# A delta-rule recurrence inside the passes of a two-block kernel: carried by a linear map of each chunk, or by three dependent products

## What is computed

```python
def rwkv7_scan(r, w, k, v, kk, bb, s0, reverse):
    def step(s, inp):
        r_t, w_t, k_t, v_t, kk_t, b_t = inp
        sa = jnp.einsum('bhij,bhj->bhi', s, kk_t)
        s = s * w_t[:, :, None, :] - sa[..., None] * b_t[:, :, None, :] + v_t[..., None] * k_t[:, :, None, :]
        return s, jnp.einsum('bhij,bhj->bhi', s, r_t)
    xs = tuple(jnp.moveaxis(t, 1, 0) for t in (r, w, k, v, kk, bb))
    s, ys = lax.scan(step, s0, xs, reverse=reverse)
    return s, jnp.moveaxis(ys, 0, 1)
```

## Time and profile before

| | us |
|---|---|
| median of three runs (3537.45 to 3548.29) | 3542.62 |
| the profiled execution, its own time | 3542.76 |
| its span | 3541.0 |
| the 12 passes, from the first product of pass 0 to the stage behind them | 660.46 |
| pass 0 | 45.03 |
| an even pass with a recurrence beside it (pass 4) | 55.42 |
| an odd one (pass 5) | 57.42 |
| pass 11 | 48.79 |

### The profile page before, as it was taken

The page is one execution under the profiler, slowest core; times in us unless marked ns, Lnnn a source line. Parts: engine busy times, 40 slices in busy tenths (PEclk is TensorE's granted clock), DMA queues, the critical chain, the costliest instruction groups (busy, mean ns, idle before and its releaser), DMA issues. The chain is left out here.

```text
span 3541.0 us, 67559 instructions
## 1 busy us (share of the span) xinstructions
PE 3073.0 (87%) x28976; PEld 2438.8 (69%) x28976; DVE 1957.7 (55%) x2743; ACT 1120.2 (32%) x1797; POOL 1042.0 (29%) x608
## 2 busy tenths in 40 slices
PE   6898898999699988999939985999999977399886
PEld 3675476887576556787828873888888856289534
DVE  3588757881287874887047703666666541421252
ACT  3223434332323443333241212343333312422222
POOL 0332133554242213454402211443434301032101
PEclk8999999999898999999969997999999988699988
DMA  9332132333232112233313321000000021121102
GB/s 351 97 93 55 32 93 71 96 95 92 61 95 73 53 49 78 84 96 91 96 46 96 109 66 74 17 21 21 3 21 21 8 81 48 39 75 60 42 1 72
DMA packets 345078, 245.48 MB, mean 69 GB/s; under 512 B 9982, under 2 KB 320948, under 8 KB 344008
## 3 DMA queue, kind: packets, MB, share of 16 engines
q1 hardware_dynamic: 340356, 231.44, 21.6%
q10 hardware_dynamic: 4420, 9.66, 0.8%
HBM read 222.27 MB, written 17.23 MB: 68 GB/s over the span
## 5 line engine op out<-in xcount | busy, mean ns | idle before, releaser
L602 POOL TENSOR_TENSOR weights_lo<-weights_raw,weights_hi 128x1024 fp32r<-128x1024 f32 (+1 forms) x234 | 593.3, 2536 | 1114.0 <-ACT weights_hi L571 1114.0
L1200 PE MATMUL psum<-moving_hi,weights_hi 128*128 128x512 f32 x1472 | 601.3, 409 | 73.4 <-DVE weights_lo L602 45.7
L1200 PE MATMUL psum<-moving_lo,weights_hi 128*128 128x512 f32 x1472 | 582.7, 396 | 0.0
L1200 PE MATMUL psum<-moving_hi,weights_lo 128*128 128x512 f32 x1472 | 582.0, 395 | 0.0
L1200 PEld LDWEIGHTS psum<-moving_hi,weights_hi 128*128 128x128 f32 x1472 | 281.6, 191 | 186.7 <-issue 60.8
L571 ACT ACTIVATE weights_hi<-weights_raw 128x1024 fp32r<-128x1024 f32 (+2 forms) x250 | 252.9, 1016 | 245.8 <-PE psum L1200 240.9
L1200 PEld LDWEIGHTS psum<-moving_hi,weights_lo 128*128 128x128 f32 x1472 | 282.0, 192 | 61.3
L1200 PEld LDWEIGHTS psum<-moving_lo,weights_hi 128*128 128x128 f32 x1472 | 282.6, 192 | 57.2 <-issue 3.8
L2632 POOL TENSOR_TENSOR second_off<-second_mats,second_masks 128x256 f32<-128x256 f32 x180 | 141.1, 786 | 183.0 <-PE psum L2077 183.0
L1200 PE MATMUL psum<-hn_hi,even_hi 128*128 128x256 f32 (+1 forms) x480 | 162.4, 338 | 27.2 <-DVE even_lo L602 27.2
L2077 PE MATMUL psum<-second_wb,second_y 64*64 64x64 f32 x2880 | 164.9, 218 | 0.0
(11 more groups left out here) (457 smaller groups left out, 6687.5 us busy)
## 6 DMA issues: line engine op xcount, KB each, us to landing
weights_raw<-in_w_up SPq DMA_DIRECT2D x88, 512.0 KB, 3.9
weights_raw<-in_w_in SPq DMA_DIRECT2D x80, 512.0 KB, 3.8
start_ada<-in_ada_w SPq DMA_DIRECT2D x12, 2048.0 KB, 18.2
odd_raw<-in_od_w_in SPq DMA_DIRECT2D x16, 1024.0 KB, 5.3
even_raw<-in_ev_w_in SPq DMA_DIRECT2D x30, 512.0 KB, 3.9
weights_raw<-in_w_down SPq DMA_DIRECT2D x32, 448.0 KB, 3.9
weights_raw<-in_w_o SPq DMA_DIRECT2D x16, 512.0 KB, 4.3
weights_raw<-in_w_down SPq DMA_DIRECT2D x16, 512.0 KB, 4.2
```

What stands on the lines that cost most here:

```text
L602: ops.tensor_tensor(self.ring.lo[i % n][:, a:b], self.ring.raw[:, t % self.ring.landing, a:b], self.ring.hi[i % n][:, a:b].bitcast(F32), A ...
L1200: return nc.tensor.matmul(to, (hi, lo)[which][:, at:at + P], moving(k)[part], start=start and k == 0 and i == 0, stop=stop and k == n_k - ...
```

## The change

The linear maps go. A new class `Steps` takes the place of `Recurrence` inside the passes. For each chunk k it has four turns, of which three hold work:

- "p": PE makes N v plus (a state) into a 64-column region, ACT first writes the state times the decay into `scaled`, then copies p out (into `wau`, as `p_sb`).
- "u": PE multiplies `wb` with `p_sb`; ACT copies the result (`u_sb`).
- "s": PE makes the new part of the state from v and `u_sb` (two products), and the output `y` (three products, one of them with the old state). DVE makes the next state by one operation with decay and `scaled`; after each fourth chunk it adds `y` into `o`.
- the fourth turn is empty.

The 48 turns are spread over slots: one after each unit, and two for each round, the first between the off-diagonal product and the place of the terms (called A below), the second behind the products of the round before (B). A pass of 15 units has 47 slots, one of 12 units has 44. So one chunk takes four slots, that is four units or two rounds. The unit "a" is made in pass 11 alone, since the `Recurrence` that still runs alone behind the passes needs it; the condition of POOL's wait is put in other words for that. Places of the terms do not move relative to the rounds; among the units they do, as there are fewer.

```diff
--- before.py
+++ after.py
@@ -2227,6 +2227,93 @@
         return range(self.items * place // places, self.items * (place + 1) // places)
 
 
+class Steps:
...
+    def pe(self, pe, what, k):
+        b, nc = self.buf, self.nc
+        n = self.order[k]
+        slot, v, g = slot_of(self.i, n), b.v_tok[:, self.i // 2 % 2, n, :], k // 4
+        state, ar = b.st[:, k % 2, :], b.ar[:, self.i % 3, n, :]
+        if what == "p":
+            if k:
+                pe.wait_ge(self.state_ready, k)
+            last = halves_matmul(nc, self.p, b.ntrk[:, slot, 0:CH], v, start=True, stop=k == 0)
+            if k:
+                last = halves_matmul(nc, self.p, ar[:, 0:CH], state, start=False, stop=True)
+            last.then_inc(self.p_ready, 1)
+        elif what == "u":
+            pe.wait_ge(self.p_taken, k + 1)
+            halves_matmul(nc, self.u, b.wb[:, slot, 0:CH], self.p_sb).then_inc(self.u_ready, 1)
+        else:
+            pe.wait_ge(self.u_taken, k + 1)
+            if k + 1 < NCH:
+                halves_matmul(nc, self.s, b.mats[:, slot, 3 * CH:], v, start=True, stop=False)
+                halves_matmul(nc, self.s, b.mats[:, slot, 2 * CH:3 * CH], self.u_sb, start=False, stop=True).then_inc(self.s_ready, 1)
+            if k % 4 == 0 and g:
+                pe.wait_ge(self.o_added, g)
+            c = n - self.starts[g]
+            y = self.y[:, c * CH:(c + 1) * CH]
+            halves_matmul(nc, y, v, b.ntrk[:, slot, CH:], start=True, stop=False)
+            if k:
+                halves_matmul(nc, y, state, ar[:, CH:], start=False, stop=False)
+            last = halves_matmul(nc, y, self.u_sb, b.mats[:, slot, CH:2 * CH], start=False, stop=True)
+            if k % 4 == 3:
+                last.then_inc(self.out_ready, 1)
+    def act(self, act, what, k):
+        b, S = self.buf, self.nc.scalar
+        if what == "p":
+            if k:
+                n = self.order[k]
+                act.wait_ge(self.state_ready, k)
+                S.activation(self.scaled, b.st[:, k % 2, :], ACT.Identity, scale=b.decay[:, self.i % 3, n:n + 1]).then_inc(self.state_scaled, 1)
+            act.wait_ge(self.p_ready, k + 1)
+            S.activation(self.p_sb, self.p, ACT.Identity).then_inc(self.p_taken, 1)
+        elif what == "u":
+            act.wait_ge(self.u_ready, k + 1)
+            S.activation(self.u_sb, self.u, ACT.Identity).then_inc(self.u_taken, 1)
+    def dve(self, dve, what, k):
+        b, V = self.buf, self.nc.vector
+        if what != "s":
+            return
+        n, g = self.order[k], k // 4
+        decay = b.decay[:, self.i % 3, n:n + 1]
+        if k + 1 < NCH:
+            dve.wait_ge(self.s_ready, k + 1)
+            if k:
+                dve.wait_ge(self.state_scaled, k)
+                V.scalar_tensor_tensor(b.st[:, (k + 1) % 2, :], self.s, decay, self.scaled, ALU.mult, ALU.add).then_inc(self.state_ready, 1)
+            else:
+                V.tensor_scalar(b.st[:, 1, :], self.s, decay, None, ALU.mult).then_inc(self.state_ready, 1)
+        if k % 4 == 3:
+            o = b.o[:, self.i // 2 % 2, self.starts[g] * CH:(self.starts[g] + 4) * CH]
+            dve.wait_ge(self.out_ready, g + 1)
+            V.tensor_tensor(o, o, self.y, ALU.add).then_inc(self.o_added, 1)
+    def due(self, slot, slots):
+        turns = self.PER_CHUNK * NCH if self.i >= 0 else 0
+        here = range(turns * slot // slots, turns * (slot + 1) // slots)
+        return [("pus"[t % self.PER_CHUNK], t // self.PER_CHUNK) for t in here if t % self.PER_CHUNK < 3]
 class Operands:
 
 
@@ -2481,7 +2568,7 @@
             over = lambda name: mask(name).unsqueeze(1).to_broadcast([P, 4, mask(name).shape[1]])
             bank = lambda b, n: psum[:, b * 512:b * 512 + 4 * n].rearrange("p (c n) -> p c n", n=n)
 
-            kinds = (["v"] if d == 0 else []) + ["tok", "kr", "br", "a", "m"]
+            kinds = (["v"] if d == 0 else []) + ["tok", "kr", "br"] + (["a"] if i == passes - 1 else []) + ["m"]
             units = [(g, what) for g in range(GROUPS) for what in kinds]
             by = ["act" if what in ("v", "tok", "a") else "dve" for _, what in units]
             taken_by = lambda n, who: by[:n + 1].count(who)
...
@@ -2511,8 +2599,10 @@
                     def beside(place):
                         for phase in terms.due(place, PLACES):
                             terms.pe(pe, phase)
-                        for item in rec.due(place, PLACES):
-                            rec.pe(pe, item)
+                    def steps(slot):
+                        for what, k in rec.due(slot, slots_of_steps):
+                            rec.pe(pe, what, k)
 
                     for n, (g, what) in enumerate(units):
                         if n >= BANKS:
@@ -2534,6 +2624,7 @@
                             else:
                                 last = halves_matmul(nc, to[:, c, :], ar[:, x, a_], bk[:, x, a_])
                         last.then_inc(unit_ready, 1)
+                        steps(n)
                         for place in after_unit(n):
                             beside(place)
                     pe.wait_ge(taken_act, by.count("act"))
@@ -2552,6 +2643,7 @@
                             for c in range(4):
                                 last = halves_matmul(nc, bank_y(n)[:, c, :], off[:, n % 2, c, :], buf.wb[:, slots(g).start + c, CH:])
                             last.then_inc(y_ready, 1)
+                        steps(len(units) + 2 * n)
                         beside(UNIT_PLACES + n)
                         if n:
                             level, g = rounds[n - 1]
...
@@ -2591,7 +2687,9 @@
                             level, g = rounds[n]
                             act.wait_ge(y_ready, n + 1)
                             S.activation(y[:, own(g), :], bank_y(n), ACT.Identity).then_inc(y_taken, 1)
+                        steps(len(units) + 2 * n)
                         beside(UNIT_PLACES + n)
+                        steps(len(units) + 2 * n + 1)
 
                 @block.vector
                 def _(dve):
...
@@ -2634,7 +2737,7 @@
 
                     for g in range(GROUPS):
 
-                        pool.wait_ge(taken_dve, taken_by(len(kinds) * (g + 1) - 3, "dve"))
+                        pool.wait_ge(taken_dve, taken_by(len(kinds) * g + kinds.index("br"), "dve"))
                         G.tensor_tensor(buf.wb[:, slots(g), 0:CH], buf.mats[:, slots(g), 0:CH], over(pre_t + "1"), ALU.mult).then_inc(wt_scaled, 1)
                         pool.wait_ge(wt_scaled, g + 1)
                         G.tensor_tensor(buf.wb[:, slots(g), 0:CH], buf.wb[:, slots(g), 0:CH], over("eye64"), ALU.add).then_inc(wt_begun, 1)
```

More of the change, by code:

```diff
@@ L2498, in products @@
             names = "unit_ready taken_act taken_dve wt_scaled wt_begun wf_begun masked y_ready y_taken w_ready w_added "
-            with stage(nc, names + Terms.NAMES + Recurrence.NAMES) as (block, sems):
+            with stage(nc, names + Terms.NAMES + Steps.NAMES) as (block, sems):
                 (unit_ready, taken_act, taken_dve, wt_scaled, wt_begun, wf_begun, masked, y_ready, y_taken, w_ready,
@@ L2502, in products @@
                 terms = Terms(sems[11:11 + Terms.COUNT], i + 1, p - 1 if d == 1 and p else None)
-                rec = Recurrence(nc, sems[11 + Terms.COUNT:], i - 1, buf, psum, eye)
+                rec = Steps(nc, sems[11 + Terms.COUNT:], i - 1, buf, psum)
+                slots_of_steps = len(units) + 2 * (len(rounds) + 1)
                 @block.sync
```

22 lines of the change are left out of this document (18 added, 4 removed).

## The result

The changed kernel takes **3489.50 us** (median of four runs, 3486.99 to 3493.69) against 3541.47 for the kernel before on the same chip; the ratio is 0.985, with a 95% interval of 0.983 to 0.987. The profiled execution took 3487.26 us.

A forecast was written before the change was run, and what follows sets the result against it. PE was taken to bound the passes. After new waits, gains of 5 x 3.1 (even), 5 x 1.7 (odd), 3.4 (pass 11) and 0.9 (pass 0) made 28.3 us off 3542.76: 3514 us, range 3490 to 3535.

The forecast's parts named there:

- 550 u: PE's work removed over passes 0 to 11, in calls of 64 columns at 0.1167 us: 64.2 us.
- The links of the even rounds: Hand-over from p to u through ACT, covered by 4 u of off-diagonal product: 0.1 us of wait each.
- The start of the rounds in an even pass: PE waits for u of chunk 5, behind DVE's state of chunk 4 and ACT's exponentials: 2.3 us.
- some 1.4 us in an even pass, 3.0 in an odd one: PE's waits in a pass of the kernel before, subtracted from the waits forecast for after.
- 0.7 us for seven such waits: Even passes: PE's small waits between p and u in the rounds, 0.7 us in all.
- The three large terms: Odd passes: waits at chunk 3's u and s (1.3 us), chunk 4's u (3.2) and the pass's end (2.3).
- PE comes to u with 28 u done: 3.2 us: Odd passes: chunk 4's copy of p stands behind ACT's exponentials, so PE waits 3.2 us more before u.
- with nothing between: Odd passes, first round: chunk 3's u and s follow directly, behind ACT's square and the round's copy: 1.3 us.
- PE's waits there at 2.3 us: End of odd passes: forward terms make DVE the slower engine, so PE waits 2.3 us.
- pass 0 (+1.1 for -0.9): Pass 0: 1.4 us of work go, POOL's wait grows by 4 u; 0.9 us gained.
- Rival 1: In the passes, waits hide each other and half of 46 us vanish: 3478.6 to 3502 us; chance 0.12.
- Rival 3: In the passes, ACT serves the round's copy before p, exposing the chain: slower, 3568 us; chance 0.09.

The follow-up runs named there:

- e1_filler: Changed kernel with the first product of y made four times instead of once in every chunk, 396 calls more; 3533.02 us.
- e9_norecip: Changed kernel with each reciprocal in VectorE's forward terms replaced by a multiply and add, so the key is not normalised; 3480.31 us.
- e10_noeye: Changed kernel with odd-pass slots realigned to the even passes' turns, and POOL's addition of the identity for the third group left out; 3472.48 us.
- e7_eye: Changed kernel with POOL's addition of the identity to the second half of wb for the third group moved to VectorE; 3493.75 us.
- e2_keep_a: Changed kernel with the unit a made again in all passes, which adds three slots to each of passes 0 to 10; 3508.32 us.
- e12_latewait: Changed kernel with odd-pass slots realigned to the even passes' turns, and two products of y ahead of the wait for u's copy; 3468.27 us.

## Why the prediction was off, step by step

**Right.** The count of 550 u (their price was 4 us too high in all); PE as the bound (e1_filler); pass 11 (44.4 with 45.4 forecast); the hand-over through ACT (0.224 for the copy against an estimated 0.25); the clock at 1.00 from pass 1 on. The links of the even rounds were priced at 0.1 us and cost 0.07. The start of the rounds in an even pass, forecast as 2.3 us, is 2.0: from the end of s of chunk 3 at 2409.65 to u of chunk 5 at 2416.57 are 6.9 us for 42 u, 4.9 us. At its end VectorE's state for chunk 5 comes at 2415.74 and p at 2415.80.

**The step that failed: the waits, on both sides of the subtraction.** The forecast set the waits of after, worked out from starts and lengths, against *"some 1.4 us in an even pass, 3.0 in an odd one"* before, which is the idle that the profile lists. Idle is counted from the end of a record, and a record ends some 0.17 us after the next product could have started. In the earlier trace rows the product at 2502.95 has 1.07 us of idle in front of it; the one ahead of it is this, of 4 u:

```profile
2501.25 0.63 PE L2077 MATMUL psum<-second_wb,second_off 64*64 64x64 f32 x16
```

It is done with at 2501.72 by its starts, so 1.23 us were lost; and the first record behind such a wait is 0.05 us longer than those that follow it, which the profile doesn't list either. Here are the waits by starts, without those at the projections of the terms, which both kernels have (passes 4 and 9, us):

| | even, forecast | even, by starts | odd, forecast | odd, by starts |
|---|---|---|---|---|
| waits before | 1.4 | 2.6 | 3.0 | 4.5 |
| waits after | 4.2 | 3.4 | 7.1 | 5.7 |
| end of the stage | not counted | 1.2, then 1.0 | not counted | 1.2, then 1.0 |

A pass thus gained 1.2 and 1.5 us over the forecast because more was there to lose, 0.8 and 1.4 because the new waits are shorter, and 0.3 at its end; the work gave 0.4 less.

**Mis-sized, even passes (3.4 us for 4.2).** *"0.7 us for seven such waits"* is 0.4 for the links of six chunks; the seventh, of chunk 4, lies in the start of the rounds, which is 2.0 for 2.3. Chunk 11 costs 0.5 for 0.6, the last level 0.2 as told, and the units 0.2 for 0.4. None of the terms is far off.

**Mis-sized, odd passes (5.7 for 7.1).** The three large terms come to 6.8 us and are 3.6. *"PE comes to u with 28 u done: 3.2 us"* left out that PE itself has work of the terms in that round. Its row stands between an off-diagonal product and the products of the round before, in pass 5:

```profile
2461.12 1.56 PE L2394 MATMUL psum<-second_tmp,table 128*128 128x256 f32 x4
...
2465.78 0.33 PE L2077 MATMUL psum<-second_wau,second_wb 64*64 64x64 f32 x4 [1.33 <-ACT second_wau L2287]
```

The projection of the squared key holds PE for 1.48 us and covers as much of the exponentials: 3.2 less 1.5 is 1.7, and 1.5 was lost by the starts (1.33 of it listed). u and s of chunk 3 *"with nothing between"*, 1.3 us, was 0.7 (0.47 listed), since the square was done before and only the copy of the round stood ahead. *"PE's waits there at 2.3 us"*, the end behind VectorE, was 0.8 by the starts and 0.83 by e9_norecip, with 0.5 more in a wait for POOL. That term came from 19.22 busy of 22.20 us; VectorE is busy 18.30 of 22.00 now and still ends only one wait of PE there: a busy share tells no wait. On the other side the sum had nothing for the first off-diagonal product (0.5 us), chunk 11 (0.6), the last level (0.2) and the links (0.5); and its terms as written add up to 7.0, not 7.1. (Pass 5 is 0.5 us longer than pass 9, between 2479 and 2488.)

**Wrong in sign, pass 0 (+1.1 for -0.9).** The wait for POOL grew as told, from 1.58 to 1.92 us. What the forecast lacked is what follows:

```profile
2210.88 0.73 PE L2077 MATMUL psum<-second_wb,second_off 64*64 64x64 f32 x16 [1.92 <-POOL second_off L2735]
2211.39 0.43 PE L2077 MATMUL psum<-second_wb,second_y 64*64 64x64 f32 x4
...
2213.10 1.07 PE L2077 MATMUL psum<-second_wb,second_off 64*64 64x64 f32 x16
```

The products run at half rate from 2211.39 to some 2214.8 (1.07 against 0.68 us), and the mean clock of the pass is 0.91 for 0.96 before. In before, after 1.58 us, they did not the earlier trace rows. In e10_noeye the wait is split into 0.92 and 0.85 us, the stretch at half rate behind it is missing, and pass 0 takes 44.88 us against 46.04 in its base. It is not the length of the wait alone: in e7_eye PE waits 2.25 us one round later (2214.78) and goes on at full rate. What else decides stays open. The Trainium skill, "TensorE: Matmul & The Clock Gate", Part 1, has the array fall back to the lower clock when it idles; the rows agree that it comes behind a wait, and don't settle when.

**The rivals.** Rival 1, that half of the 46 us of waits vanish, named the right side, and its band of 3478.6 to 3502 holds the result; 0.12 was too little for it. Its reason, that waits hide each other, is shown at one place only, by e7_eye and e10_noeye. The larger part was that the waits of before had been read too small, some 13 us over the ten passes, and those of after too large, some 11. The rest is smaller: the shorter ends of the stages 3 us and pass 11 one, less 4 us by the price of the work and 2 by pass 0. Rival 3, the chain exposed, has its price in an even pass of e2_keep_a, though not by its route (the exponentials stand ahead of p there, not the copy of the round): 56.82 us, slower than before's 55.42. The change was one round away from it.

## What to carry to other kernels

Before pricing a wait on a chain, list everything that the waiting engine itself has at that place, including its share of unrelated stages, and measure the waits of before and of after in the same way, by the starts of the products: the idle that the profile lists was 0.17 us short at each, and leaves the small restarts out. Where a chain shares a queue with a long block, the place of each link against that block can be worth more than the link's length: here moving the links gave 3.4 us in an odd pass, moving a part of the block 0.7. A wait that the profile names may lie in the shadow of a second one that ends at the same time; take the work away without adding it elsewhere before counting on the gain.

## What the runs showed of the hardware beyond that

A product behind a wait that is only just over starts 0.02 us late, and the product behind it another 0.05; the profile lists neither as idle. Such small gaps, of 0.02 to 0.15 us, are 34 in an even pass of the changed kernel with 1.6 us together, some of them behind projections and not behind waits; before they were 12 with 0.7. Where the copy had come earlier, as in front of s in e12_latewait, nothing was lost.

An operation of 128x256 on POOL takes 0.73 us, and about twice that beside some of VectorE's. In an even pass of the changed kernel, POOL's first two rows and VectorE's third overlap so:

```profile
2409.39 0.73 POOL L2741 TENSOR_TENSOR second_wb<-second_mats,second_masks 128x256 f32<-128x256 f32 x1 [2.25 <-DVE second_mats L2713]
2410.20 1.53 POOL L2743 TENSOR_TENSOR second_wb<-second_wb,second_masks 128x256 f32<-128x256 f32 x1
```

```profile
2410.20 0.95 DVE L2485 TENSOR_TENSOR second_e<-second_cum 128x768 f32<-128x768 f32 x1
```

POOL's operation ends 0.58 us after VectorE's. The Trainium skill, "SBUF — State Buffer", section on the two separate sides, has GpSimd and a VectorE operation with two inputs in SBUF share a port pair, which the first of them holds for the whole instruction; these rows agree. Beside VectorE's operations with one input in PSUM (2409.56, 2409.86) POOL took 0.73.
